# The last six token tiles of y computed as three pairs with seven block products each, in a one-core layer kernel

## The reference, cut to what matters

```python
def rmsnorm(x, w):
    xf = x.astype(jnp.float32)
    y = xf * lax.rsqrt(jnp.mean(xf * xf, axis=-1, keepdims=True) + NORM_EPS) * w.astype(jnp.float32)
    return y.astype(x.dtype)
...
    branch_m = hm @ w_pm.astype(x.dtype)
...
    merged = jax.nn.sigmoid(g_m) * branch_m + jax.nn.sigmoid(g_a) * branch_a
    y = merged @ w_out.astype(x.dtype)
    return x + rmsnorm(y, post_w)
```

## Time and profile before

| | us |
|---|---|
| median of 3 runs | 1371.56 |
| the profiled execution | 1369.94 |
| its span | 1368.1 |
| TensorE busy | 1352.3 |
| VectorE busy | 794.5 |
| ScalarE busy | 641.7 |
| GpSimd busy | 569.2 |

### The profile page before, as it was taken

How to read it: one execution, slowest core, us unless ns; L and a number is a source line. 1 busy time by engine, 2 the same in 40 slices (tenths; PEclk the granted TensorE clock), 3 DMA queues, 4 the chain that set the end, 5 groups by cost and what they waited for, 6 DMA issues and landing times.

```text
span 1368.1 us, 18779 instructions
## 1 busy us (share of the span) xinstructions
PE 1352.3 (99%) x6470; PEld 1127.3 (82%) x6470; DVE 794.5 (58%) x1260; ACT 641.7 (47%) x1320; POOL 569.2 (42%) x400
## 2 busy tenths in 40 slices
PE   7999999999999999999999999999999999999998
PEld 5788888888888888888888888888888888888786
DVE  5874438346543835877756575755644442997632
ACT  6644543543444455345445445544544553533421
POOL 5253435335443534654434445344333544454000
PEclk9999999999999999999999999999999999999999
DMA  6132233324233323455442634345343354966421
GB/s 194 51 76 65 69 74 90 96 48 126 76 85 72 84 79 61 149 173 144 114 145 66 188 104 134 100 127 175 87 150 97 93 188 165 345 200 196 183 97 58
DMA packets 210462, 165.02 MB, mean 121 GB/s; under 512 B 32400, under 2 KB 186544, under 8 KB 210368
## 3 DMA queue, kind: packets, MB, share of 16 engines
q1 hardware_dynamic: 210224, 163.75, 40.5%
q10 hardware_dynamic: 144, 0.07, 0.0%
HBM read 117.41 MB, written 40.08 MB: 115 GB/s over the span
## 4 chain that ended last, share of the span: by engine, by line
PE 91%; DVE 4%; issue 2%; ACT 1%; DMA 1%; SPq 1%; POOL 0%; DVEq 0%; POOLq 0%; ACTq 0%
PE proj L1244 69%; PE side L1189 3%; PE proj L1189 2%; PE side L1289 2%; PE side L1268 2%; PE side L1345 2%; PE side L1354 2%; PE proj L1170 2%; PE side L1170 2%; PE side L1277 1%; PE side L1317 1%; PE side L1350 1%; PE side L1300 1%; DMA x_sb<-x_in 1%; PE side L1362 1%
## 5 line engine op out<-in xcount | busy, mean ns | idle before, releaser
L1080 POOL TENSOR_TENSOR w_lo<-raw,w_hi 128x512 fp32r<-128x512 f32 x161 | 234.5, 1458 | 413.8 <-ACT w_hi L1456 413.7
L1244 PE MATMUL proj<-hi_T,w_hi 128*128 128x512 f32 x832 | 338.1, 406 | 2.2 <-ACT snap L1474 1.6
L1244 PE MATMUL proj<-hi_T,w_lo 128*128 128x512 f32 x832 | 325.2, 391 | 0.0
L1244 PE MATMUL proj<-lo_T,w_hi 128*128 128x512 f32 x832 | 324.1, 390 | 0.0
L1244 PE MATMUL proj<-hi_B,w_hi 128*128 128x512 f32 x624 | 254.1, 407 | 5.6 <-ACT b_sb L1518 4.0
L1244 PE MATMUL proj<-hi_B,w_lo 128*128 128x512 f32 x624 | 244.2, 391 | 0.0
L1244 PE MATMUL proj<-lo_B,w_hi 128*128 128x512 f32 x624 | 243.6, 390 | 0.0
L1080 POOL TENSOR_TENSOR w_lo<-s_sb,w_hi 128x512 fp32r<-128x512 f32 x104 | 156.7, 1510 | 153.5 <-ACT w_hi L1456 153.4
L1244 PEld LDWEIGHTS proj<-hi_T,w_hi 128*128 128x128 f32 x832 | 156.4, 188 | 36.0 <-issue 3.5
L1244 PEld LDWEIGHTS proj<-hi_T,w_lo 128*128 128x128 f32 x832 | 156.1, 188 | 34.2
L1244 PEld LDWEIGHTS proj<-lo_T,w_hi 128*128 128x128 f32 x832 | 156.6, 188 | 30.4
(11 more groups left out here) (253 smaller groups left out, 2014.5 us busy)
## 6 DMA issues: line engine op xcount, KB each, us to landing
raw<-w_in SPq DMA_DIRECT2D x95, 512.0 KB, 6.0
m_spill<-stage SPq DMA_DIRECT2D x16, 1024.0 KB, 5.6
chunk<-m_spill SPq DMA_DIRECT2D x32, 512.0 KB, 3.8
gate_spill<-stage SPq DMA_DIRECT2D x8, 1024.0 KB, 4.3
gst<-gate_spill SPq DMA_DIRECT2D x32, 256.0 KB, 3.2
share<-share_spill SPq DMA_DIRECT2D x12, 512.0 KB, 5.0
x_sb<-x_in SPq DMA_DIRECT2D x8, 512.0 KB, 7.6
hm_spill<-stage SPq DMA_DIRECT2D x4, 1024.0 KB, 8.8
```

What stands on the lines that cost most here:

```text
L1080: TT(w_lo_ring[k % RING][:], src, w_hi_ring[k % RING][:].bitcast(F32), ALU.subtract).then_inc(lo_pool, 1)
L1244: mm = pe.matmul(acc(p, which), w[:, kt, :], m[:, kt, :], start=(first and kt == 0 and w is wh and m is h_hi[b]), stop=(kt == 3 and w is w ...
```

## The change

Tiles 0 and 1 of y are computed as before, both in the PSUM tensor `side`. Tiles 2 to 7 become three pairs of kind "y", handled like the projection pairs with seven products: the stationary blocks come out of `merged` (two token tiles), the moving ones are blocks of w_out: B11, B21, B22 are slices of out_hi and out_lo, and T1 to T4 are differences of blocks, loaded again from w_out by six transfers of 1 MB and made as whole blocks of 128x2048 (`block_sums` on VectorE, `block_high` on ScalarE, low parts of T1 and T3 on GpSimd, of T2 and T4 on VectorE). The result of a pair lands in y_sb in SBUF; `pair_squares` on ScalarE squares it there, `pair_result` on VectorE ends it. x is loaded again into two slots inside merged, each once its tokens have been split or used. Some semaphores are merged (row_sq, mean_sq, root).

```diff
@@ -152,9 +154,13 @@
     NM = len(pairs)
     seq = plan_products(0, NP) + [(t, WHOLE) for t in range(KT)] + plan_products(NP, NM - NP)
     NK = len(seq)
+    NY = NM + (NT - YD) // 2
+    pairs += [Pair("y", i, Tile("y", 0, YD + 2 * i), Tile("y", 0, YD + 2 * i + 1)) for i in range(NY - NM)]
+    seq += plan_products(NM, NY - NM)
     no = {v: i for i, v in enumerate(seq)}
     FIRST_M = next(p for p in range(NP) if pairs[p].kind != "att")
-    pair_of = {(q.kind, q.head): p for p, q in enumerate(pairs) if q.kind != "att"}
+    pair_of = {(q.kind, q.head): p for p, q in enumerate(pairs) if q.kind not in ("att", "y")}
     def att_pair(h, kind, g):
         return 5 * h + next(i for i, two in enumerate(HEAD_PAIRS) if (kind, g) in two)
@@ -326,6 +332,8 @@
             act_late[min(at + 4, NK)].append(("out_hi", i, j))
             dve_late[(at + 4, NK - 1, NK, NK)[i]].append(("out_lo", i, j))
     sp_late[NK - 1].append(("post_in",))
+    for b, at in (("T1", no[last, "P7"] + 1), ("T2", NK), ("T4", NK), ("T3", NK + 1)):
+        sp_late[at].append(("block_in", b))
     act_late[NK - 2].append(("merged_hi", 0, 0))
     dve_late[NK - 2].append(("merged_lo", 0, 0))
     act_late[NK].append(("merged_hi", 0, 1))
...
+        def moving(p, b, kt):
+            if pairs[p].kind != "y":
+                return h_hi[b][:, kt, :], h_lo[b][:, kt, :]
+            if b in t_hi:
+                return t_hi[b][:, kt, :], t_lo[b][:, kt, :]
+            row, columns = (kt if b == "B11" else 4 + kt), half_of(b == "B22")
+            return out_hi[row // 2][:, row % 2, columns], out_lo[row // 2][:, row % 2, columns]
+        def block_wait(eng, b):
+            eng.wait_ge(block_low if b in ("T1", "T3") else block_lo, 1 if b in ("T1", "T2") else 2)
...
+                elif what == "block_in":
+                    b = it[1]
+                    w = {(k, c): w_out[k * HALF:(k + 1) * HALF, half_of(c)].rearrange("(k p) s -> p k s", p=P)
+                         for k in range(2) for c in range(2)}
+                    if b == "T4":
+                        sp.wait_ge(mg_done, 16)
+                    else:
+                        sp.wait_ge(pe_prod, no[NM - 1, {"T1": "P7", "T3": "P4", "T2": "P3"}[b]] + 1)
+                    first, less = {"T1": (w[0, 1], w[0, 0]), "T3": (w[0, 1], w[1, 1]), "T2": (w[1, 1], None),
+                                   "T4": (w[1, 0], None)}[b]
+                    sp.dma_start(t_sum[b][:], first).then_inc(block_in[b], 16)
+                    if less is not None:
+                        sp.dma_start(t_less[b][:], less).then_inc(block_in[b], 16)
...
+            order = list(range(YD)) + [t for i in range(YD, NT, 2) for t in (i + 1, i)]
             def x_again(t):
-                if t < 4:
-                    sp.wait_ge(mg_done, 13 + t)
+                if t < YD:
+                    sp.wait_ge(mg_lo, 2 * t + 2 if t < 2 else t + 3)
                 else:
-                    sp.wait_ge(y_done, t - 3)
-                sp.dma_start(gst[t % 4][:], x[t * P:(t + 1) * P, :]).then_inc(x2_in[t % 4], 16)
-
-            for t in range(4):
+                    sp.wait_ge(y_done, order.index(t - YD) + 1)
...
+            def block_low_part(b):
+                g.wait_ge(block_hi, ("T1", "T2", "T4", "T3").index(b) + 1)
+                if b == "T1":
+                    g.wait_ge(block_sum, 2)
+                TT(t_lo[b][:], t_sum[b][:], t_hi[b][:].bitcast(F32), ALU.subtract).then_inc(block_low, 1)
+            def y_parts(p):
+                add(p, "S1")
+                add(p, "S2")
+            y_parts(NM)
+            for k in range(NK, NK + LEAD + 1):
+                if not low_dve[k]:
+                    low(k)
+            y_root(0)
+            block_low_part("T1")
+            y_root(1)
+            block_low_part("T3")
+            for i in range(2, YD):
+                y_root(i)
+            for k in range(NK, len(seq)):
+                if NK + LEAD < k + LEAD < len(seq) and not low_dve[k + LEAD]:
+                    low(k + LEAD)
+                p, name = seq[k]
+                if name == "P5" and p < NY - 1:
+                    y_parts(p + 1)
+                if name in ("P4", "P3") and p < NY - 1:
+                    y_root(YD + 2 * (p - NM) + (name == "P3"))
+            for i in range(NT - 2, NT):
+                y_root(i)
         @block.tensor
...
                     product(k)
                 for kt in HT2_ORDER if k == 1 else ():
                     second_half(kt)
-            for t in range(NT):
+            for t in range(YD):
                 output_tile(t)
+            for k in range(NK, len(seq)):
+                product(k)
         @block.scalar
...
+            def pair_squares(k):
+                p, name = seq[k]
+                j, half, done = {"P2": (0, 0, c11_done), "P7": (1, 1, c22_done), "P4": (1, 0, c21_done),
+                                 "P3": (0, 1, c12_done)}[name]
+                t = pairs[p].tiles[j].part
+                act.wait_ge(done, p + 1)
+                squares[0] += 1
+                act.wait_ge(row_sq, SQ_Y + squares[0] - 1)
+                A(y_junk[:], y_sb[t][:, half_of(half)], ACT.Square, scale=0.5 * DM ** -0.5,
+                  accum_out=ysq[:, t, half:half + 1]).then_inc(row_sq, 1)
+            squares = [2 * YD]
+            def block_high(b):
+                act.wait_ge(block_sum, ("T1", "T2", "T4", "T3").index(b) + 1)
+                A(t_hi[b][:], t_sum[b][:], ACT.Copy).then_inc(block_hi, 1)
...
-            for t in range(NT):
-                if t + 2 < NT:
+            for k in range(NK, NK + LEAD + 1):
+                high(k)
+            HIGHS = (("T1", "T2", "T4"), ("T3",))
+            for t in range(YD):
+                y_squares(t, 0)
+                y_squares(t, 1)
+                if t + 2 < YD:
                     merged_high(t + 2, 0)
-                for half in range(2):
-                    y_squares(t, half)
+                for b in HIGHS[t]:
+                    block_high(b)
+            for k in range(NK, len(seq)):
+                p, name = seq[k]
+                after(k)
+                if k + LEAD > NK + LEAD and k + LEAD < len(seq):
+                    high(k + LEAD)
+                if name in ("P2", "P7", "P4", "P3"):
+                    pair_squares(k)
         @block.vector
...
+            def with_x(t, part):
+                rows_ = y_sb[t][:].rearrange("p (k c) -> p k c", c=P)[:, part, :]
+                STT(rows_, rows_, yrs[:, t:t + 1], x_slot(t)[:, part, :], ALU.mult, ALU.add).then_inc(y_done, 1)
+            def pair_result(p, j, at_):
+                t = pairs[p].tiles[j].part
+                last = at_ == NT - 1
+                first, second = (0, 3) if j == 0 else (1, 2)
+                dve.wait_ge(row_sq, SQ_Y + 2 * YD + 4 * (p - NM) + second + 1)
+                STT(ysum[:, t:t + 1], ysq[:, t, 0:1], EPS, ysq[:, t, 1:2], ALU.add, ALU.add).then_inc(mean_sq, 1)
+                columns = half_of(1) if j == 0 else slice(0, DM)
+                step(STT(y_sb[t][:, columns], y_sb[t][:, columns], 0.5, pw_sb[:, columns], ALU.mult, ALU.mult))
+                dve.wait_ge(root, ROOT_Y + at_ + 1)
+                dve.wait_ge(x_in[t], 32)
+                for part in (slice(0, 4), slice(4, 8)) if last else (slice(0, KT),):
+                    with_x(t, part)
+            def block_sums(b):
+                dve.wait_ge(block_in[b], 32 if b in t_less else 16)
+                if b in ("T2", "T4"):
+                    dve.wait_ge(block_sum, 1 if b == "T2" else 2)
+                if b == "T4":
+                    ins = TT(t_sum[b][:], t_sum[b][:], t_sum["T2"][:], ALU.subtract)
+                elif b == "T2":
+                    ins = TT(t_sum[b][:], t_sum[b][:], t_sum["T1"][:], ALU.subtract)
+                else:
+                    ins = TT(t_sum[b][:], t_sum[b][:], t_less[b][:], ALU.subtract)
+                ins.then_inc(block_sum, 1)
+            def block_low_part(b):
+                dve.wait_ge(block_hi, ("T1", "T2", "T4", "T3").index(b) + 1)
+                TT(t_lo[b][:], t_sum[b][:], t_hi[b][:].bitcast(F32), ALU.subtract).then_inc(block_lo, 1)
             for part in range(2):
                 merged_low(1, part)
-            for t in range(NT):
-                if t + 2 < NT:
-                    merged_low(t + 2, 0)
-                result(t)
+            add(NM, "S3")
+            result(0)
+            block_sums("T1")
+            block_sums("T2")
+            block_sums("T4")
+            block_low_part("T2")
+            block_sums("T3")
+            result(1)
+            for k in range(NK, len(seq)):
+                if NK + LEAD < k + LEAD < len(seq) and low_dve[k + LEAD]:
+                    low(k + LEAD)
+                p, name = seq[k]
+                after(k)
+                if name == "P6":
+                    add(p, "S4")
+                if name == "P7" and p < NY - 1:
+                    add(p + 1, "S3")
+                if k == NK + 1:
```

(8 more changed lines are left out.)

184 lines of the change are left out of this document (102 added, 82 removed).

## The result

The changed kernel takes 1388.97 us (median of 4, 1388.51 to 1390.85), the kernel before 1371.17 us beside it: ratio 1.0136, 95% interval 1.0124 to 1.0148. Forecast were 1384.3 us and a range up to 1389. The sign was right, the size 5 us too small, and the ratio times 1371.56 us, 1390.2 us, lies above the range. The span of the profiled execution is 1386.7 us for 1368.1.

The account below looks back on a forecast made before the run. TensorE, busy 99%, was taken as the bound: -8.16 us of matmuls + 4.27 + 5.95 + 1.7 + 3.95 + 0.8 + 2.75 + 1.45 = +12.7 us, 1382.6 us profiled, 1384.3 us as median; range 1374 to 1389.

Parts of the forecast that it names:

- 1 matmuls: All three pairs of y: 84 matmuls per pair for 96, 36 fewer in all, -8.16 us.
- Step 2: Tile 0 of y: GpSimd operations take turns with VectorE ahead of merged_lo(0,1), so row block 6 starts later, +4.27 us.
- step 3: First P6: TensorE waits for the snapshot of P1, behind x, VectorE's block sums and T3's high part, +5.95 us.
- step 4: First P7: TensorE waits for the snapshot of P6, behind GpSimd's long low part of T3 and C11, +1.7 us.
- Step 5: P7 of the other two pairs: VectorE finishes a whole tile before P3's sum; wait 1.97 each, +3.95 us.
- 6 last P4: Last pair: no P1 stands between P7 and P4, so P4 waits for the snapshot of P7, +0.8 us.
- step 7: End of y: work behind the last matmul takes 5.96 us for 3.21, GpSimd's root hidden beside the product, +2.75 us.
- Step 8: Clock: TensorE falls to a granted clock of 0.50 behind the long stop in tile 0, +1.45 us.
- Rival D: TensorE's clock falls at more stops, also those of 2 us, and before P6: 3 to 5 us more, 1388; chance 0.07.
- A: Rival at first P6 and P7: GpSimd's long operation blocks only 1.08 us, -4.9 us, 1379.3; chance 0.14.
- B: Rival for y: no VectorE-GpSimd lock for these operands and no clock loss, -1.5 us, 1370.1; chance 0.08.
- C: Rival at first P6: T blocks and x come early enough, T3 summed by 1300; -4.6 us, 1367.0; chance 0.07.

Follow-up runs that it names:

- filler run: The changed kernel with matmuls that nobody reads put on TensorE at its stops (16 before row block 6, 22 before first P6, 10 before later P7s): 1385.60 us, ratio 1.0104.

## Why the prediction was wrong

Step by step, predicted and in the two profiles:

| step | predicted | measured |
|---|---|---|
| 1 matmuls | -8.16 | -8.16 |
| 2 tile 0 | +4.27 | +4.21 (4.34 + 0.48 - 0.61 of before) |
| 3 first P6 | +5.95 | +4.90 |
| 4 first P7 | +1.7 | 0 (0.11, counted in step 8) |
| 5 P7 of the other pairs | +3.95 | +5.67 |
| 6 last P4 | +0.8 | +0.94 |
| 7 end | +2.75 | +3.41 |
| 8 clock | +1.45 | +7.73 (2.88, 1.73, 1.72, 1.06, 0.34 around P4) |
| sum | +12.7 | +18.7 |

From the start of out_lo to the last y_sb the second profile is 18.7 us longer, so nothing is left over. Of the 6.0 us above the forecast, 3.12 are slow clock behind the later pairs' stops and around P4, 1.43 more slow clock behind tile 0, 2.4 steps 5 and 7; steps 3 and 4 with the slow clock behind P6 took 1.0 less.

**Step 8 failed.** It counted one fall, behind the stop in tile 0, with 1.45 us, and put the falls behind the stops of 2 us and more at nothing, since the trace had one long stop of 3.98 us and no row for stops of 2 to 3. The runs show falls behind such stops too: 7.73 us of slow clock for 1.45. That the one behind the first P6 costs nothing of its own was right: it took the place of step 4's wait. Rival D named the right mechanism, falls at more stops, with a chance of 0.07, 3 to 5 us more and 1388; it should have been part of the forecast. The filler run shows that the idle time is the cause, and the run with two GpSimd operations shows it in the kernel before, where no other part of the change is. The loss differs from execution to execution: behind the same stop of 4.3 us in tile 0, over the same 84 matmuls, eight profiles lose 1.47 to 2.88 us, and three stops of 2.83 to 3.22 us have no fall behind them. I have no row that says why. So the mechanism is shown, and the 7.73 us are the size of one execution.

**Step 2 held, but not as a term of its own.** The out_lo rows, the order of turns and 4.27 us were right, shown in the kernel before alone. The prediction added it to step 3. The run with GpSimd started later shows that taking step 2 away mostly lengthens step 3: the end of the chain behind it sets P6, and that chain came only 1.7 us sooner.

**Steps 3 and 4** were right in mechanism and sum less: 7.65 predicted, 4.90 stop and 1.73 slow clock measured. The snapshot was expected ready at 1312.5 and was at 1314.1, TensorE at 1306.6 and came at 1309.4, since tile 0 ran at half clock (its half result was squared from 1291.70, not 1290.4). Then the slow clock behind P6 covered the wait at P7 but for 0.11 us: TensorE was ready for P7 at 1321.25, and the chain at 1321.36. That the two met so closely is luck. The long operation's 4.3 us is 4.4 in the rows, so A and B are out. By the Trainium skill (SBUF — State Buffer, section "SBUF: two separate sides"), whoever starts first locks the shared pair of ports for the whole instruction; the 6.71 us row agrees.

**Step 5 and step 7 were mis-sized**, by 0.86 us a stop and 0.66 at the end, and most likely by one thing. The working took a root of 0.55 us hidden beside the product. With both operands in SBUF the product locks the root out, and VectorE then waits 0.51 us for it at each of two tiles, in each pair and at the end. The size fits; no run takes these waits away and leaves the rest. That most of both steps is an order that could be other is shown (0.77 a stop and 4.72 at the end); the prediction put it at 0.76 each without the queueing at P4 and without the 1.08, and kept it for a rival. That the two numbers agree is partly luck, as in the run the root's lock was still there.

**C** failed by its own sign: T3's sum ends at 1311.7, not by 1300.

## What to carry to other kernels

Price a stop of TensorE of 2 us and more with a slow stretch behind it, and shorten such stops before anything else. In the profiles of y here, 30 of 33 stops of 1.98 us and more in which TensorE stood idle had one, for 1.1 to 3.0 us each; of the stops up to 1.55 us none had. That is a count, not a limit of the hardware. Where VectorE is full, GpSimd work on SBUF is not free: it took 4.4 us of VectorE's time where VectorE needs 2.28, so moving it back to VectorE can gain. And add up the work of both engines between two points on TensorE's path before pricing stops one by one: a budget that does not fit moves from wait to wait, and here only more time under other matmuls ended it.

## What the runs showed of the hardware that I had not expected

- Stops of 1.98, 2.18 and 2.29 us were followed by a granted clock of 0.50 as most of the long ones, stops of 1.55, 1.47 and 1.34 by none; and yet it stayed at 1.00 behind stops of 2.83, 2.84 and 3.22 us. Slow intervals (0.42 us and more) began at the restart in some cases, 0.3 to 1.8 us behind it in others.
- With only ScalarE's order changed, five executions gave 1383.8, 1384.6, 1388.9, 1389.4 and 1390.8 us, the first two at a mean clock of 0.993, the others at 0.988 to 0.990. Falls behind its 1.98 us stops in some executions alone would give that spread, and the stop of 2.83 us with and without a fall in two runs makes it likely; only one of the five has a trace, so it is not shown.
- GpSimd holds the port 4.4 us for a 128x2048 fp32 subtraction that takes VectorE 2.28, and a 128x1 root lasts 0.93 or 1.46 us beside a product of two SBUF operands, for 0.55 beside one that reads PSUM.
